# Feed-forward layers with the norm factor on the gate's half only, and behind the output projection for the other half

## What is computed

```python
def rmsnorm(x, g):
    xf = x.astype(jnp.float32)
    y = xf * lax.rsqrt(jnp.mean(xf * xf, axis=-1, keepdims=True) + NORM_EPS)
    return (y * g.astype(jnp.float32)).astype(x.dtype)

def swiglu(x, w_in, w_out):
    a, b = jnp.split(x @ w_in, 2, axis=-1)
    return (jax.nn.silu(a) * b) @ w_out
...
    for l in range(DEPTH):
        x = x + 0.5 * swiglu(rmsnorm(x, ffn1_norm[l]), w_ffn1_in[l], w_ffn1_out[l])
        u = rmsnorm(x, mix_norm[l])
...
        x = x + merged @ w_out[l]
        x = x + 0.5 * swiglu(rmsnorm(x, ffn2_norm[l]), w_ffn2_in[l], w_ffn2_out[l])
    return rmsnorm(x, final_norm)
```

## Time and profile before

| | us |
|---|---|
| median of 3 runs | 2360.81 |
| lowest and highest | 2360.24, 2362.17 |
| the profiled execution, its own time | 2363.54 |
| its span, first to last instruction | 2361.6 |
| TensorE busy | 2337.7 (99%) |
| TensorE weight loads | 2278.6 (96%) |
| VectorE busy | 1637.2 (69%) |
| ScalarE busy | 1278.4 (54%) |
| GpSimd busy | 354.1 (15%) |
| mean granted TensorE clock | 0.998 |

### The profile page before, as it was taken

The page is one execution under the profiler, slowest core; times in us unless marked ns, Lnnn a source line. Parts: engine busy times, 40 slices in busy tenths (PEclk is TensorE's granted clock), DMA queues, the critical chain, the costliest instruction groups (busy, mean ns, idle before and its releaser), DMA issues.

```text
span 2361.6 us, 50717 instructions
## 1 busy us (share of the span) xinstructions
PE 2337.7 (99%) x21742; PEld 2278.6 (96%) x21742; DVE 1637.2 (69%) x2260; ACT 1278.4 (54%) x1831; POOL 354.1 (15%) x303
## 2 busy tenths in 40 slices
PE   9999999999999999999999999999999999999998
PEld 8999999999999999999999999989999999989998
DVE  6765787976667657878666766776766666776763
ACT  6654655654455456565555544645544554636554
POOL 4011020300200210203003002431002002431001
PEclk9999999999999999999999999999999999999999
DMA  6555433555555544335555655422545555422553
GB/s 252 196 197 180 178 125 133 186 198 189 195 189 196 197 178 179 124 130 191 200 186 189 223 179 197 157 91 89 213 175 198 204 179 197 168 80 91 216 179 124
DMA packets 57679, 410.20 MB, mean 174 GB/s; under 512 B 6384, under 2 KB 6640, under 8 KB 8688
## 3 DMA queue, kind: packets, MB, share of 16 engines
q1 hardware_dynamic: 56592, 402.15, 47.3%
q10 hardware_dynamic: 864, 4.82, 0.5%
HBM read 405.89 MB, written 1.05 MB: 172 GB/s over the span
## 4 chain that ended last, share of the span: by engine, by line
PE 83%; DVE 7%; ACT 4%; issue 4%; POOL 1%; DMA 1%; SPq 0%; DVEq 0%; ACTq 0%; POOLq 0%
PE bank L556 83%; DVE sb_wlo L512 3%; DVE area L1837 1%; ACT sb_whi L504 1%; DMA sb_raw<-stream 1%; PE bank L2185 1%; ACT area L1557 0%; DVE area L1820 0%; DVE area L1786 0%; DVE area L646 0%; POOL sb_x_ssq L699 0%; ACT area L1623 0%; ACT area L1578 0%; DVE area L1894 0%; ACT area L1581 0%
## 5 line engine op out<-in xcount | busy, mean ns | idle before, releaser
L556 PE MATMUL bank<-area,sb_whi 128*128 128x256 f32 x11752 | 2022.7, 278 | 4.5 <-ACT area L780 1.8
L556 PEld LDWEIGHTS bank<-area,sb_whi 128*128 128x128 f32 x11752 | 1772.8, 188 | 15.4 <-issue 4.2
L556 PE MATMUL bank<-area,sb_wlo 128*128 128x256 f32 x5876 | 1610.8, 278 | 5.3 <-DVE sb_wlo L512 5.0
L504 ACT ACTIVATE sb_whi<-sb_raw 128x1024 fp32r<-128x1024 f32 x762 | 792.8, 1055 | 604.4 <-PE bank L556 590.8
L556 PEld LDWEIGHTS bank<-area,sb_wlo 128*128 128x128 f32 x5876 | 1095.9, 188 | 8.0 <-DVE sb_wlo L512 7.9
L512 DVE TENSOR_TENSOR sb_wlo<-sb_raw,sb_whi 128x1024 fp32r<-128x1024 f32 x762 | 955.1, 1265 | 165.5 <-ACT sb_whi L504 163.7
L646 DVE TENSOR_TENSOR area<-bank,sb_x_diag 128x512 f32<-128x512 f32 x244 | 167.2, 686 | 70.3 <-PE bank L556 49.8
L979 DVE TENSOR_TENSOR area<-area,area 128x256 f32<-128x256 f32 x176 | 76.3, 434 | 189.6 <-ACT area L930 188.8
L556 PE MATMUL bank<-area,area 64*64 64x64 f32 (+5 forms) x2864 | 149.6, 249 | 0.1
L556 PEld LDWEIGHTS bank<-area,area 64*64 64x64 f32 (+3 forms) x2864 | 127.4, 139 | 19.1 <-ACT area L1605 5.3
L691 POOL TENSOR_TENSOR sb_x_ssq<-sb_x 128x256 f32<-128x256 f32 x9 | 12.0, 1331 | 853.1 <-DVE sb_x L1018 842.9
(11 more groups left out here) (269 smaller groups left out, 1179.4 us busy)
## 6 DMA issues: line engine op xcount, KB each, us to landing
sb_raw<-stream SPq DMA_DIRECT2D x379, 1024.0 KB, 4.8
sb_raw<-stream SPq DMA_DIRECT2D x4, 512.0 KB, 7.3
area<-lora ACTq DMA_DIRECT2D x2, 768.0 KB, 6.7
area<-c ACTq DMA_DIRECT2D x1, 1504.0 KB, 7.2
sb_x<-x SPq DMA_DIRECT2D x4, 256.0 KB, 5.3
area<-mem ACTq DMA_DIRECT2D x1, 1024.0 KB, 9.6
out<-sb_x SPq DMA_DIRECT2D x4, 256.0 KB, 2.9
area<-m ACTq DMA_DIRECT2D x1, 512.0 KB, 5.5
```

The costliest lines, as they stand in the source:

```text
L504: e.activation(k.hi[k.slot[p]], raw_piece(k, p), ACT.Copy).then_inc(*k.done("weights_hi", p))
L556: return e.matmul(out, lhsT, rhs, start=start, stop=stop, skip_group_check=True, tile_position=at)
```

## The change

The scaling multiplies only the gate's half, into a tile `m.gate`. The gating multiply reads the other half unscaled from the bank. So the mark that a unit leaves on its bank is "hidden" (done by the gating multiply), no longer "scaled". Behind the output projection a new multiply by the factors writes `m.out`, and the residual add reads that tile instead of the bank, after a wait for it. The tiles take the place of `m.ab`.

```diff
@@ ffn_tiles
-    m.ab = [area(k, at + 2 * T * i, 2, T) for i in range(3)]
+    m.gate = [area(k, at + T * i, T) for i in range(3)]
+    m.out = [area(k, at + T * i, T) for i in range(3, 5)]
@@ tensor_ffn
     for i in range(NF):
-        mark = ("scaled", s, i)
+        mark = ("hidden", s, i)
@@ scalar_gate
     e.wait_ge(*k.when("scaled", s, i))
-    e.activation(m.st[i % 3], m.ab[i % 3][:, 0, :], ACT.Silu).then_inc(*k.done("silu", s, i))
+    e.activation(m.st[i % 3], m.gate[i % 3], ACT.Silu).then_inc(*k.done("silu", s, i))
@@ vector_scaled
     if i == 0:
         e.wait_ge(*k.when("factors", s))
-    scaled_pair(e, k, ("scaled", s, i), m.ab[i % 3])
+    e.wait_ge(*k.when("product", "hidden", s, i))
+    b = bank_at(k, "hidden", s, i)
+    e.tensor_tensor(m.gate[i % 3], b[:, 0:T], k.sx.rs, ALU.mult).then_inc(*k.done("scaled", s, i))
@@ vector_gated
     e.wait_ge(*k.when("silu", s, i))
-    e.tensor_tensor(m.ht[i % 3], m.st[i % 3], m.ab[i % 3][:, 1, :], ALU.mult).then_inc(*k.done("hidden", s, i))
+    b = bank_at(k, "hidden", s, i)
+    e.tensor_tensor(m.ht[i % 3], b[:, T:2 * T], m.st[i % 3], ALU.mult).then_inc(*k.done("hidden", s, i))
@@ vector_ffn
         b = bank_at(k, "x", s, j)
         e.wait_ge(*k.when("product", "x", s, j))
-        e.scalar_tensor_tensor(k.x[:, j, :], b[:, 0:T], 0.5, k.x[:, j, :], ALU.mult, ALU.add).then_inc(
+        e.tensor_tensor(m.out[j % 2], b[:, 0:T], k.sx.rs, ALU.mult).then_inc(*k.done("out_scaled", s, j))
+        e.wait_ge(*k.when("out_scaled", s, j))
+        e.scalar_tensor_tensor(k.x[:, j, :], m.out[j % 2], 0.5, k.x[:, j, :], ALU.mult, ALU.add).then_inc(
             *k.done("x", s, j))
```

## The result

| | before | after |
|---|---|---|
| median, us (4 runs each, taken together) | 2360.52 | 2374.34 |
| lowest and highest | 2359.54, 2362.17 | 2372.77, 2377.35 |
| profiled execution: time, span | 2363.54, 2361.6 | 2372.77, 2371.0 |

The ratio is 1.006, 95% interval 1.0048 to 1.0072: the change costs 13.8 us. The forecast was +6.7, so the direction was right and the size was half of what came. 2374.34 lies inside the range, where the rival "slower pace after a wait" had its place (2370 to 2378).

A forecast was written before the change was run, and what follows sets the result against it. TensorE, busy 99% of the span, was taken to bound the kernel. Added waits of 2.2 + 2.9 + 0.7 + 0.5 + 0.5 = 6.8, rounded down to 6.7 us, on 2360.8 gave 2367.5 us; range 2364.3 to 2376.5.

The forecast's parts named there:

- slower pace after a wait: Rival: new waits start TensorE's slow pace in B0f2, B1f2 and A0f1; total +9 to +18 us; chance 0.20.
- VectorE's time is worth nothing: Feed-forward steady state: the shorter scaling takes 48 us off VectorE, but nothing waits for it; value 0.
- Banks in B0f2 and B1f2: Unit 3 waits 1.01 us for the gating multiply, plus 0.1 for restart; two stages, 2.2 us.
- Banks in A0f1: Waits for the gating multiply at units 4, 10, 17, 18: 0.71, 1.33, 0.22, 0.22 us; 2.9 us with restarts.
- Unit 3 is just in time: A0f1: TensorE's unit 3 gets its bank without a wait, so no term was added.
- The value chosen for the multiply: A0f1, unit 4: the gating multiply takes 0.42 us since it reads a bank; wait 0.71 us, with 1.00 it is 1.29.
- Column 7: Last output projection column: chain grows 0.47 us; costs 0.7 us in four openings, 0.5 in B0f1, 0.5 at the end.
- The four other openings: Stage starts behind the last column, B0f1 aside: 0.08 us uncovered plus 0.1 for restart, four times, 0.7 us.
- the waits as summed, pace and clock unchanged: Likeliest case: only the summed waits come, TensorE's pace and clock stay; 2365.8 to 2368.6 us, chance 0.52.
- The clock: Rival: TensorE's granted clock falls after each of four new waits; +6 us, 2373 us; chance 0.05.
- Faster: Rival: relieved VectorE delivers low weight parts at 24.85 and 1303.56 in time; -7.2 us, about 2355.5 us; chance 0.04.

The follow-up runs named there:

- release_only: Kernel before, with only the bank's mark moved from the scaling to the gating multiply, the scaling still 128x512; 2373.11 us.
- out_only: Kernel before, with only the added multiply by the factors behind the output projection and the wait for it; 2361.59 us.
- four_banks: Changed kernel, with four banks in turn instead of three in the feed-forward stages; 2362.31 us.
- one_wait: Kernel before, with unit 3 of B0f2 and B1f2 made to wait for the gating multiply of unit 0; 2365.77 us.
- waits_elsewhere: Kernel before, with unit 3 of A0f2, A1f1, A1f2 and B1f1 made to wait for the scaling of unit 2; 2376.90 us.
- after_reset: Changed kernel, with six extra float32 128x128 matmuls on constants into an unused bank, in A0f1, B0f1, B0f2 and B1f2; 2375.82 us.
- four_banks_turned: Changed kernel, with four banks in turn in the feed-forward stages, the rotation beginning one bank further on than in four_banks; 2363.96 us.
- four_banks_early: Changed kernel, with four banks as in four_banks and, in B0f1, one high weight part and its low part made earlier; 2364.54 us.
- before_four_banks: Kernel before, with only four banks in the feed-forward stages, in the rotation of four_banks_turned; 2359.57 us.

## Why the prediction was right, and where it fell short

**VectorE's time is worth nothing**: right. TensorE's list ran no faster anywhere in steady state, and the gating multiplies behind the late factors start as long after the scaling as before (3.63 us at unit 0 of A0f1).

**Banks in B0f2 and B1f2**: right in place, chain and size. Forecast 1.11 us with restart each; the matmul behind came 1.28 and 1.16 us later. The reading that SiLU's table load, not the scaling, sets the time held.

**Banks in A0f1**: units 4 and 10 came as forecast, 0.84 us (0.81) and 1.47 (1.43). Units 17 and 18 came too, 0.23 us each with restart (0.32); as each holds the weight load for 0.18 us and the matmul for less, the list of the matmuls' waits doesn't have them. "Unit 3 is just in time" hangs on the execution: it holds with the fallen clock from 25 to 29 us (0.57) and not without it, as release_only shows (1.11 us). The forecast had that clock in its rows, but took the margin at unit 3 from that one execution.

The value chosen for the multiply, 0.42 instead of 1.00 us, was the right one, and the traces bear out the reason. The Trainium skill ("SBUF — State Buffer", "SBUF: two separate sides") names two conditions: the VectorE instruction has two SBUF inputs, and a GpSimd instruction that reads SBUF has started first. Here are both kinds of multiply behind the same GpSimd sum, which began 0.12 to 0.13 us ahead: two SBUF inputs in out_only, a bank and one in four_banks.

```profile
46.29 0.80 POOL L699 TENSOR_TENSOR area<-area,area 128x256 f32<-128x256 f32 x1
46.42 0.96 DVE L979 TENSOR_TENSOR area<-area,area 128x256 f32<-128x256 f32 x1
...
45.28 0.80 POOL L704 TENSOR_TENSOR area<-area,area 128x256 f32<-128x256 f32 x1
45.40 0.41 DVE L991 TENSOR_TENSOR area<-bank,area 128x256 f32<-128x256 f32 x1
```

0.96 against 0.41 us. Over the twelve profiles, the multiplies with two SBUF inputs behind a GpSimd instruction with at least 0.15 us left took 0.48 to 1.25 us, 22 of 22; those that read a bank took 0.41 to 0.43 us, 17 of 17, the one at 37.94 above among them. The order counts as well: in release_only the multiply with two SBUF inputs took 0.42 us (36.26), as the sum began 0.20 us behind it.

**Column 7**: the end is exact, +0.45 of 0.47, and B0f1 is too, 0.46 of 0.47, though its wait for GpSimd is 0.35 us, not 0.6. The four other openings were put too low, 0.18 us each. In out_only they cost 0.35 each; after the change A1f1 and B1f1 cost that and the two mixers 0.15. At A1f1 the wait with its restart took 0.21 us, near the forecast, and the rest came behind it within some 5 us, at the slow pace.

**The step that failed** is "the waits as summed, pace and clock unchanged", with chance 0.52. The waits themselves were right: 4.8 + 0.5 + 1.6 + 0.45 = 7.3 us in the bill, against 6.8. The pace was not unchanged: the forecast expected 8.9 matmuls per us in B0f2 and named growth of B0f2 and B1f2 by more than 2 us each as a sign of being wrong; there were 8.54, and the two grew by 3.3 and 3.2 us. The terms for what follows a wait held the restart alone, 0.1 us, and the loss by pace, which measured 6.1 us, was put into a rival with 0.20, because "no reason for the two paces is visible". But the trace of before held evidence: of the two waits for a low part near the start of a feed-forward stage, both were followed by a slow stretch, though the first of them also by a fallen clock (0.57 from 25 to 29 us).

Counted over the profiles of after, release_only, one_wait, waits_elsewhere and after_reset, there are 16 waits for a VectorE area of 0.88 us or more that follow a stretch at 113 to 114 ns a matmul; behind 14 of them the matmuls took 117.7 ns. B0f2 and B1f2 in the eight profiles without such a wait there (before among them) show no long slow stretch, 16 of 16. The pace is not bound to such a wait, though. In release_only TensorE makes 133 matmuls in the 16 us from 1624 on, where before made 141, with no wait of over 0.15 us in the 8 us ahead; and behind the four waits of 0.97 us in front of mixers (four_banks, four_banks_turned, four_banks_early) the slow pace lasted 8 to 13 us only.

With the 6.1 us of slow pace the sum would have been 6.7 + 6.1 = 12.8; 13.8 came. The forecast's own rival had the size: up to 4.2 us in B0f2 and in B1f2 and 2.6 in A0f1, against 2.0, 2.0 and 2.1. That closeness is luck to an extent, as the paces differ between executions of one kernel.

**The clock** did not fall behind a new wait: 0.998 over the span and 1.00 in every stretch there. **Faster** did not come: the wait for the low part at B0f1 is still 0.42 us, since it hangs on ScalarE's high part, as argued.

## What to carry to other kernels

When a change moves the last reader of a PSUM bank, look at the places where the reader is late (behind table loads and factor computations), not at steady state: one more bank in the rotation removed the waits, but the next user's first bank then has to be checked as well. A wait in a busy matmul stream should be priced at its length plus, as a likely case, a slow stretch behind it, here 2 to 4 us for 1 us of waiting. And where a profile of before shows both paces, count how often a wait precedes the slow one before giving that rival a chance.

## What was not expected of the hardware

TensorE has two paces at one granted clock (1.00, so the 2.4 GHz level): 113.3 and 117.7 ns for a 128x256 matmul with its weight load, 4% apart, in the same code and at the same busy share. Waits of 0.88 to 1.19 us in mid-stream stood ahead of the slow one in 14 of 16 cases, waits of 0.42 to 0.74 us for B0f1's low part in 8 of 12 profiles. Behind the 14 and the 8 the slow pace held for 37 to 117 us. Its end came at the same place in different executions: 467 matmuls behind the wait in B0f2 and B1f2 after the change and in B1f2 of one_wait, 440 behind that of B0f1 in release_only, one_wait and before_four_banks; where it ran on, it lasted about to the output projection (944 to 995 matmuls). By the Trainium skill ("TensorE: Matmul & The Clock Gate", "Back-to-back issue gap") isolated matmuls of 256 columns would start about 256 / 2.4 + 2.5 = 109 ns apart, an estimate from its formula, which leaves the weight load out; every matmul here has one, and the trace has neither pace at that value.

What the slow pace is, and what ends it, stays open. It isn't the clock, and an irregular matmul didn't end it. Whether DMA traffic or the order of weight loads sets it was not tested.
